# A layer's FFN with the up projection multiplied by seven products over its whole contraction, and the down projection in chunks of two pairs summed in device memory

## What is computed

```python
def conv_ffn(h, w_up, conv_w, conv_b, w_down):
    up = depthwise_conv(h @ w_up, conv_w, conv_b, FFN_CONV // 2)
    g, v = jnp.split(up, 2, axis=-1)
    return (jax.nn.gelu(g, approximate=True) * v) @ w_down
...
    hx2 = modulate(rms_norm(x, g_ffn_pre[l]), sh2, sc2)
    x = x + gt2 * rms_norm(conv_ffn(hx2, w_up[l], conv_ffn_w[l], conv_ffn_b[l], w_down[l]), g_ffn_post[l])
```

## Time and profile before

| what | value |
|---|---|
| median of 3 runs | 2086.96 us (2085.97 to 2090.21) |
| the profiled execution, its device time | 2088.77 us |
| its span, first to last instruction | 2087.0 us |
| PE busy | 98% of the span |
| DVE busy | 73% |
| ACT busy | 39% |
| mean granted TensorE clock | 0.995 |

### The profile page before, as it was taken

One profiled execution on the slowest core, in us unless ns is written; L12 is line 12 of the kernel. 1 busy time (PEld: TensorE's weight loads), 2 busy tenths in 40 slices (PEclk: granted clock), 3 DMA queues, 4 the chain that ended last, 5 costly groups with the idle time before them and its releaser, 6 DMA issues.

```text
span 2087.0 us, 28299 instructions
## 1 busy us (share of the span) xinstructions
PE 2054.5 (98%) x11682; PEld 1755.4 (84%) x11682; DVE 1528.3 (73%) x2203; ACT 812.1 (39%) x1078; POOL 78.7 (4%) x145
## 2 busy tenths in 40 slices
PE   7999999999999999999999999999999999999998
PEld 4678887888777888988889898898988888888887
DVE  5567978876889886776858676676776768577577
ACT  5346576543333352333424243242333424233243
POOL 0000000001110000000000000000000000000002
PEclk9999999999999999999999999999999999999999
DMA  9953424434886524333343433334333333333343
GB/s 393 408 213 111 145 92 168 136 112 155 328 286 238 172 91 142 101 122 121 102 141 102 131 111 105 128 111 132 107 117 124 102 128 103 99 101 101 101 180 104
DMA packets 86193, 311.19 MB, mean 149 GB/s; under 512 B 9456, under 2 KB 13552, under 8 KB 84016
## 3 DMA queue, kind: packets, MB, share of 16 engines
q1 hardware_dynamic: 67824, 243.09, 34.1%
q0 software_dynamic: 17424, 65.50, 9.5%
q10 hardware_dynamic: 816, 0.79, 0.1%
HBM read 300.95 MB, written 8.39 MB: 148 GB/s over the span
## 4 chain that ended last, share of the span: by engine, by line
PE 68%; DVE 2%; DMA 1%; issue 1%; ACT 0%; DVEq 0%; ACTq 0%
PE bank L1010 22%; PE bank L1011 22%; PE bank L1012 22%; DMA ada_raw<-in_adabg 1%; DVE w_lo L1554 0%; DVE acc L2191 0%; PE bank L1330 0%; PE bank L1121 0%; DVE ada_acc L1586 0%; DMA w_raw<-in_stream 0%; DVE x L1894 0%; ACT h_hi L622 0%; DVE prod L1905 0%; DVE ss L1562 0%; PE bank L1335 0%
## 5 line engine op out<-in xcount | busy, mean ns | idle before, releaser
L1010 PE MATMUL bank<-h_hi,w_hi 128*128 128x512 f32 (+1 forms) x1968 | 709.1, 360 | 4.5 <-ACT y_lru L691 1.1
L1011 PE MATMUL bank<-h_lo,w_hi 128*128 128x512 f32 (+1 forms) x1968 | 705.7, 359 | 0.0
L1012 PE MATMUL bank<-h_hi,w_lo 128*128 128x512 f32 (+1 forms) x1968 | 704.1, 358 | 0.0
L1554 DVE TENSOR_TENSOR w_lo<-w_raw,w_hi 128x1024 fp32r<-128x1024 f32 x260 | 315.9, 1222 | 151.2 <-ACT w_hi L622 150.6
L1010 PEld LDWEIGHTS bank<-h_hi,w_hi 128*128 128x128 f32 x1968 | 370.4, 188 | 62.6 <-issue 11.8
L622 ACT ACTIVATE w_hi<-w_raw 128x1024 fp32r<-128x1024 f32 x260 | 273.2, 1056 | 383.0 <-DMA w_raw<-in_stream 383.0
L1012 PEld LDWEIGHTS bank<-h_hi,w_lo 128*128 128x128 f32 x1968 | 370.4, 188 | 57.0
L1011 PEld LDWEIGHTS bank<-h_lo,w_hi 128*128 128x128 f32 x1968 | 370.7, 188 | 47.6
L1010 PE MATMUL bank<-act_hi,w_hi 128*128 128x512 f32 (+1 forms) x688 | 265.1, 385 | 1.8 <-DVE acc L2163 1.5
L1011 PE MATMUL bank<-act_lo,w_hi 128*128 128x512 f32 (+1 forms) x688 | 264.3, 384 | 0.0
L1012 PE MATMUL bank<-act_hi,w_lo 128*128 128x512 f32 (+1 forms) x688 | 264.3, 384 | 0.0
(11 more groups left out here) (340 smaller groups left out, 2704.4 us busy)
## 6 DMA issues: line engine op xcount, KB each, us to landing
w_raw<-in_stream SPq DMA_DIRECT2D x340, 512.0 KB, 3.5
ada_raw<-in_adabg POOLq DMA_DIRECT2D x112, 512.0 KB, 4.5
ada_raw<-in_ada SPq DMA_DIRECT2D x64, 512.0 KB, 13.8
x<-in_x_t SPq DMA_DIRECT2D x4, 1024.0 KB, 8.4
acc<-in_adabg SPq DMA_DIRECT2D x8, 512.0 KB, 6.0
x<-in_x_t POOLq DMA_DIRECT2D x4, 1024.0 KB, 8.8
x_kept_d<-x SPq DMA_DIRECT2D x4, 1024.0 KB, 5.6
c<-in_ctx_t SPq DMA_DIRECT2D x2, 1024.0 KB, 14.2
```

Of the source, the lines that this page charges most:

```text
L1010: t.matmul(out, w, v, start=start, stop=False)
L1011: t.matmul(out, w, v_l, start=False, stop=False)
L1012: return t.matmul(out, w_l, v, start=False, stop=stop)
L1554: v.tensor_tensor(lo_unit(n), raw_unit(n), hi_unit(n).bitcast(F32), ALU.subtract).then_inc(lo_done, 1)
```

## The change

- The up projection of pairs 4 to 43 uses seven products for all 16 feature tiles: four units of `seven_products` and none of `four_tiles`. The token sums are made for all eight couples of tiles (upper four couples first), in place in `acc` (one of them in `kick_raw`), with `t_lo` in the same room. `acc` is thereby taken until the last up unit. DVE no longer waits for `x1_kept` there; ACT does.
- DVE makes block sums for every up unit (three sets of room for them, `SETS`), and the ring has five slots throughout.
- The down projection goes in 20 chunks of two pairs, and a last one of four. Chunks 0 and 1 run whole behind pairs 4 and 5; from pair 6 to pair 41 eight tiles (half a chunk) run behind every pair, none behind pairs 42 and 43. A tile is 2 x 3 matmuls of 512 tokens. A unit of down weights holds four tiles.
- A finished tile is no longer added by DVE: ACT copies it from PSUM to one of four staging places (`take_down`), and POOL issues a DMA to device memory, a plain one for chunk 0 and one that accumulates after that (`add_down`). ACT may write a staging place again when the DMA from it has landed (`tile_moved`), and PE may write the bank when ACT has copied (`down_added`).
- In `seven_products` PE waits bank by bank for the copies of the tiles behind the pair before.
- The convolution is split in `convolve_gate` and `convolve_value` with other work between; `common_sums` of a pair waits for the pair's last unit where it waited for the third.
- At the end SP reads the sums back to `acc` (`load_sums`, 4 x 1 MB, after the last up unit is used), ahead of the four kept units.

```diff
-        WSUM[UP[_c, _p] + 1], WSUM[UP[_c, _p] + 2] = 0, 1
+QUADS = ((4, 5), (6, 7), (0, 1), (2, 3))
+SETS = 3
+WSUM = {UP[_p] + _w: 4 * (_p - CH) + _w for _p in range(CH, FT) for _w in range(4)}
...
+            def load_sums():
+                sp.wait_ge(*used(LAST_DOWN - 1))
+                for i in range(4):
+                    sp.wait_ge(tile_moved[i], 16 + 16 * (TILES // 4))
+                for i in range(4):
+                    sp.dma_start(acc[:, ds(4 * i * L, 4 * L)].rearrange("p (k l) -> p k l", k=4), acc_d[:, 4 * i:4 * i + 4, :]).then_inc(quarter_in[i], 16)
...
+                if n == UNITS - KEPT:
+                    load_sums()
                 load_unit(n)
...
+            def add_down(t, c, m):
+                pool.wait_ge(down_added, t + 1)
+                if c == 0:
+                    pool.dma_start(in_stage(acc_d[:, m, :]), stage(t % 4)).then_inc(tile_moved[t % 4], 16)
+                else:
+                    pool.wait_ge(tile_moved[t % 4], 16 + 16 * (t // 4))
+                    pool.dma_start(in_stage(acc_d[:, m, :]), stage(t % 4), accum_op=ALU.add).then_inc(tile_moved[t % 4], 16)
...
+            def take_down(n, t):
+                act.wait_ge(down_done, t + 1)
+                if t >= 4:
+                    act.wait_ge(tile_moved[t % 4], 16 + 16 * (t // 4))
+                a.activation(stage(t % 4), in_stage(bank[DOWN_BANK(n, t)][:, :]), ACT.Copy).then_inc(down_added, 1)
+            taken = 0
+            for n in range(CH, FT):
+                u, d = UP[n], AFTER_UP[n]
+                seeds_of(n - 1)
+                hi(u + 3)
+                gelu_of(n - 1)
+                hi(u + 4, u + 5)
+                round_of(n - 1)
+                hi(u + 6)
+                copy_first(n)
+                for unit in d:
+                    for t in range(taken, taken + 2):
+                        take_down(n, t)
+                    hi(unit + 3)
+                    for t in range(taken + 2, taken + 4):
+                        take_down(n, t)
+                    taken += 4
...
+                def bank_free(i):
+                    if first and free:
+                        pe.wait_ge(down_added, free - i)
...
+                    if ab == 0:
+                        bank_free(3)
+                    product(alone_v[:, 0:H], block_of(n, 6 + ab), t_of(q, 2), first and ab == 0, last and ab == 1)
+                    if ab == 0:
+                        bank_free(2)
+                    product(common[:, 0:H], block_of(n, ab), b11, first and ab == 0, False)
+                    if ab == 0:
+                        bank_free(1)
+                    product(alone_g[:, 0:H], block_of(n, 2 + ab), b21, first and ab == 0, False)
...
-            dve.wait_ge(x1_kept, 16 * 4)
-            for q in range(4):
-                k = KT // 2 + 2 * q
+            for half in range(2):
+                q0 = 4 - 4 * half
+                for q in range(q0, q0 + 4):
...
+            for n in range(CH, FT):
+                u, d = UP[n], AFTER_UP[n]
+                lo(u + 2)
+                if n > CH:
+                    if not AFTER_UP[n - 1]:
+                        common_sums(n - 1)
+                    pair_sums(n - 1)
+                sum_blocks(u + 3)
+                convolve_gate(n - 1)
+                lo(u + 3)
+                sums_if(u + 4)
+                convolve_value(n - 1)
+                lo(u + 4)
+                sums_if(u + 5)
+                multiply(n - 1)
+                lo(u + 5)
+                split_act(n - 1, (n - 1) % CH)
+                sums_if(u + 6)
+                for unit in d:
+                    sums_if(unit + 3)
+                    lo(unit + 2)
+                    if unit == d[0] and n in ADA_PAIRS:
+                        eat_ada(1)
+                    if unit == d[-1]:
+                        common_sums(n)
```

More of the change, by code:

```diff
@@ L92 @@
 BY_PE = 2 * len(SUM_BANK)
-DOWN_TILE = {DOWN[_c] + _u: KT * _c + 2 * _u + 2 for _c in range(NCH) for _u in range(KT // 2)}
 COUNT = {}
@@ L928, in gelu_of, with round_first @@
                 a.activation(cg[:, n % 2, :], cg[:, n % 2, :], ACT.Gelu_apprx_tanh).then_inc(ffn_gelu, 1)
+            def round_first(half):
+                q0 = 4 - 4 * half
+                act.wait_ge(*used(UP[FIRST] + 1 + 2 * half))
+                a.activation(first_of_two(h_hi[:, 2 * q0:2 * q0 + 8, :]), quarters_of[:, q0:q0 + 4, 1, :], ACT.Copy).then_inc(t_rounded, 1)
             for n in range(FIRST):
@@ L1389, in four_tiles, with product, seven_products @@
                 mm.then_inc(unit_used, 1)
-            def seven_products(n, w, b):
+            def product(out, block, x, start, stop):
+                return three(out, *block, *x, start, stop)
+            def seven_products(n, w, b, free):
                 alone_g, alone_v, common, parts = (bank[i] for i in b)
@@ L1395, in seven_products @@
                 _, high, low = sums_of(n)
-                def product(out, block, x, start, stop):
-                    return three(out, *block, *x, start, stop)
+                first, last = w == 0, w == 3
                 def sum_block(i, ab):
@@ L1410, in seven_products @@
[L1410 to L1421 removed]
+                    q = QUADS[w][ab]
@@ L1440, in down @@
[L1440 to L1454 removed]
+                    pe.wait_ge(t_ready, 3)
+                elif not AFTER_UP[n - 1]:
+                    pe.wait_ge(sum_v, n - 1 - CH)
@@ new lines, in up_pair, with down @@
+                for w in range(4):
+                    if n == CH and w == 2:
+                        pe.wait_ge(t_ready, 4)
+                    seven_products(UP[n] + w, w, UP_BANK(n), TILES_BY[n - 1] if n > CH and AFTER_UP[n - 1] else 0)
+            def down(n, taken):
+                if n == CH:
+                    pe.wait_ge(conv_v, CH)
+                else:
+                    pe.wait_ge(sum_v, n - CH)
+                if n in FFN_SUM:
+                    sum_ada(FFN_SUM[n], bank[7])
+                for i, (c, m) in enumerate(down_after(n)):
+                    t, u = taken + i, DOWN[c, m]
+                    pe.wait_ge(ffn_split, TWO * c + TWO)
+                    if m % 4 == 0:
+                        pe.wait_ge(lo_done, u + 1)
+                    if i >= 4:
+                        pe.wait_ge(down_added, t - 3)
+                    if i == 3 and n in FFN_SUM:
+                        pe.wait_ge(ada_read, FFN_SUM[n] + 1)
+                    for k in range(TWO):
+                        q = (TWO * c + k) % CH
+                        mm = three(bank[DOWN_BANK(n, t)][:, :], *block_of(u, TWO * (m % 4) + k), act_hi[:, q, :], act_lo[:, q, :],
+                                   k == 0, k == TWO - 1)
@@ L1455, in down @@
                     mm.then_inc(down_done, 1)
             for i, kg in enumerate((2, 3, 0, 1)):
[L1458 to L1465 removed]
+                four_tiles(UP[FIRST] + i, kg, UP_BANK(3), KT // 2, KT // 2 - 1)
+            for n in range(CH, FT):
+                up_pair(n)
+                if AFTER_UP[n]:
+                    down(n, TILES_BY[n - 1] if n > CH else 0)
@@ new lines, in sums_if @@
+            def sums_if(n):
+                if n in WSUM:
+                    sum_blocks(n)
+            for n in range(CH, FT):
+                u, d = UP[n], AFTER_UP[n]
[16 more added lines that the diff above has]
+                for unit in d:
+                    if unit == d[0] and n in FFN_SUM:
+                        take_ada(FFN_SUM[n], bank[7])
+                    sums_if(unit + 3)
[3 more added lines that the diff above has]
+                    if unit == d[-1]:
+                        common_sums(n)
@@ L2282 @@
         stream[OUT_H[m][0]], stream[OUT_H[m][1]] = w_out[m]
-    for c in range(NCH):
-        stream[DOWN[c]:DOWN[c] + 8] = w_down[c]
+    for c in range(CHUNKS):
+        for m in range(0, KT, 4):
+            stream[DOWN[c, m]] = by_two[c, m // 4]
+    stream[LAST_DOWN:] = by_four
     both = np.stack([w_up[:FIRST], w_up[FT:FT + FIRST]]).reshape(2, FIRST, 2, P, 2, 4 * P)
```

425 lines of the change are left out of this document (179 added, 246 removed).

## The result

The changed kernel takes 2229.34 us, median of 4 runs (2226.05 to 2242.32), beside 2086.94 us for the kernel before on the same chip: 1.0691 times as long, 95% interval 1.067 to 1.0713. Forecast were 2063 us and a range up to 2108. Rival A is what happened, and larger than its upper end.

A forecast was written before the change was run, and what follows sets the result against it. PE's matmul issue rate was taken to bound the kernel. Terms -53 + 2 + 3 + 2 + 12 + 2 + 8 = -24 us, against the median of 2086.96, gave 2063 us; range 2046 to 2108.

The forecast's parts named there:

- Rival A: Accumulating DMA lands late, holding ACT's copies and PE's 7th matmul of the next pair; 2107 to 2118 us, chance 0.29.
- the tiles' transfers: Accumulating DMAs of down tiles behind pairs: PE waits 0.1 us a pair, 3 us in all (0 to 58).
- L: Time from ACT's copy of a down tile to the landing of its DMA; put at 4.8 us.
- upper bound of 6.5: Highest landing time taken: load and store in a row, 3.3 + 2.2 + 0.3, and 0.7 for a stream load.
- The formula: PE waits not at all up to a copy-to-landing time of 4.9 us; beyond, 36 us for each us, over 36 pairs.
- The gain: Up projection, pairs 4 to 43: 48 matmuls of 512 become 84 of 256, 1.33 us a pair, 53 us saved.
- 2 off for pairs 42 and 43: No down tiles there to hide behind; DVE has 20.7 us of work for 19.1, costing 2 us (0 to 4).
- VectorE in the steady part: DVE's work per pair, 26.2 of 30.0 us, stays ahead of PE and costs nothing.
- The start: PE waits for DVE: 6.4 us ahead of pair 3, 4.6 at pair 4, 1 after; together 12 (8 to 15).
- The clock: A stall of 6 us at the start may lower the granted clock; 2 us (0 to 4).
- The end: After the last up unit, 4 MB of sums delay the kept units; pair 43's chain shows 2 us; 8 (5 to 11).
- C: Start and end hidden better than thought, with the low ends of all terms; 2047 us, chance 0.08.

The follow-up runs named there:

- experiment 4: Changed kernel with its 304 accumulating transfers taking the same bytes from a constant area in pieces of 2 KB instead of 1 KB; 2132.7 us, 1.0213 of the kernel before.
- experiment 5: Changed kernel with all 304 additions run from a constant area, so ACT need not wait for landings; 2051.82 us, 0.9821 of the kernel before.
- experiment 1: Changed kernel without the 304 accumulating transfers and the waits of ACT and GpSimd for them; 2051.93 us, 0.9825 of the kernel before.
- experiment 6: Changed kernel, whole computation, with eight down tiles behind a pair made four behind its second and four behind its fourth unit, one pair later; 2062.07 us, 0.9876.

## Why the prediction was wrong

**The term that failed is the tiles' transfers**, "L = 4.8, at the edge", 3 us with bounds 0 to 58. It measured 176 us (1362.6 - 1186.5). The mechanism was the right one and stood there as rival A: a landing holds a copy, the copy a bank, the bank PE's matmul of the next pair. For the first transfer of a burst L came out as forecast, 4.9 us. But the path goes through the second, and its L is 7.9, beyond the upper bound of 6.5. That bound was a load and a store in a row for one transfer on a busy queue, and its rows were of the wrong kind. The last step put an accumulation nearest to a 512 KB load by GpSimd because it moves as many bytes. No row of before had an addition in it, and an addition takes 2.4 to 2.9 times a store's engine time. What was left out is that more additions of 2.0 us of all engines each are under way before the second has landed. A bound has to be built for the burst.

**The formula gave the first part of the cost, and the holes brought more.** From the start of copy 1 to the start of copy 5 is the copy's own 0.60 and L, with less than 0.1 from the landing to the next copy. Over the 36 bursts it is 8.62 us on average in the changed kernel and 6.50 in experiment 4, so L is 8.0 and 5.9 (in the runs where ACT does not wait it is 5.44 from start to start, ACT's own pace). The formula gives 36 x 3.1 = 112 us and 36 x 1.0 = 36; measured were 176 and 82 (1268.5 - 1186.5). It lacks two things. In experiment 4 copy 6 starts within 0.2 us of the landing of the third transfer in all 36 bursts, so that landing and not the second's is the one that ends last: copy 6 ends 9.6 us after copy 1 where 8.0 costs nothing, which is 59 us. And in the changed kernel the granted clock is 0.96 on average from 800 to 2153, 0.04 x 1353 = 54 us at most. PE's waits for ACT's copies come to 94.9 us in 74 places there and to 55.7 in 41 in experiment 4. The rest of either is the slower pace of some pairs, some 10 us, and open.

**The gain** is there: -50.4 in the middle without additions. The middle has 39 of the 40 pairs, 52 of the 53 us, and the forecast took 2 off for pairs 42 and 43: -50. A pair takes 30.0 us as forecast, of it 168 matmuls in 19.0 and 48 in 10.9.

**VectorE in the steady part** cost nothing, as forecast: in the window 1300 to 1500 of experiment 5 it is busy 161 of 200 us, 81%, and PE never waits for it there.

**The start** was forecast at 12 + 2, and with pair 4's gain of 1.3 in that stage at 12.7. It measures 7.8, and 6.5 in experiment 1. Its steps, in the changed kernel:

```profile
744.22 0.80 PE L1081 MATMUL bank<-h_hi,w_hi 128*128 128x512 f32 x1 [6.39 <-DVE w_lo L1633]
...
770.43 0.36 PE L1081 MATMUL bank<-kick_hi,w_hi 128*128 128x256 f32 x1 [2.31 <-DVE sums_lo L1631]
776.02 0.39 PE L1081 MATMUL bank<-t_hi,w_hi 128*128 128x256 f32 x1 [0.55 <-DVE sums_lo L1631]
```

6.4 ahead of pair 3 came as 6.39. The 4.6 ahead of pair 4 came as 2.31 and the 1 behind it as 0.55. The clock took the 2 us that were set down for it: it is 0.66 from 744.2 to 750, which is 2.0 us of 5.8. And PE came to pair 3 at 737.8, 2.7 us ahead of the 740.5 of the kernel before; why is not shown, and it hides a part of the cost.

**The end** was forecast at 8 us (5 to 11) and measures 5.4 in the changed kernel and 7.1 in experiment 1. It came as forecast. ACT, VectorE and PE behind the last up unit, which is used by 2153.07:

```profile
2167.00 1.06 ACT L680 ACTIVATE h_hi<-x 128x1024 fp32r<-128x1024 f32 x1 [4.46 <-DMA x<-in_stream]
```
```profile
2168.09 1.22 DVE L1633 TENSOR_TENSOR h_lo<-x,h_hi 128x1024 fp32r<-128x1024 f32 x1 [3.08 <-ACT h_hi L680]
```
```profile
2163.32 0.50 PE L1081 MATMUL bank<-act_hi,w_hi 128*128 128x512 f32 x1 [1.88 <-DVE act_lo L2081]
...
2174.67 0.36 PE L1081 MATMUL bank<-act_hi,w_hi 128*128 128x256 f32 x1 [2.94 <-DVE acc L2239]
```

The kept units landed in 12.8 us in place of 6.7. ACT stood 4.5 us for the first, and its roundings ended 18.7 us after 2153.07, in the 18 to 21 of the forecast; VectorE stood for ACT, and PE for VectorE's addition of a last tile, 2.9 us. The wait of 1.9 is the chain of pair 43, forecast at 2.

**The spread of chances.** Rival A had 0.29, worked from an L of up to 6.5. C had 0.08, and 2052 us without the additions is near its 2047. The bounds of 0 to 58 us, for an operation that no row showed, were the widest of the sum and still did not hold. The range's upper end also does not follow from its own sum: at L = 6.1 the term is 43 us and the time 2103, and 2108 belongs to an L of some 6.2.

## What to carry to other kernels

A DMA that adds into memory is not a store with a little more: before a kernel leans on its landing, count its engine time for the burst in which it comes, not for one alone. Where only its landing hurts, the cure is not fewer transfers but more time until the buffer is written again; the same 304 additions were worth -1.2% when they came four at a time, and +6.9% eight at a time.

## What the runs showed of the hardware

- An accumulating DMA of 256 KB into device memory takes all 16 engines 1.65 us with pieces of 2 KB and 2.02 with pieces of 1 KB, a plain store 0.69. GpSimd is held 0.88 and 1.19 us by its issue, and 0.72 by the store's. From the end of the copy the first of a burst lands after 4.5 and 4.9 us, the second after 5.8 and 7.9; the stores after 2.9 both.
- Of the additions with pieces of 1 KB (272 packets each) at most three are under way: each of the 304 is issued after the third one back has landed. With pieces of 2 KB (144 packets, experiment 4) four were under way after 176 of the issues. The cause is open.
- A DMA share of 0.90 over 200 us beside a PE that is busy 200 of 200 costs PE nothing, as long as nothing waits for a landing (experiment 5).
- Holes of 1.8 and 1.5 us on PE were followed by windows of 2 us with a granted clock of 0.55 and 0.60, and starts 0.21 us apart, the lower level of 1.2 GHz for most of them. With two holes a pair in the changed kernel the mean granted clock from 800 to 2153 is 0.96, with one a pair in experiment 4 it is 0.99 from 800 to 2058; experiments 1, 5 and 6, nearly without holes, had 1.00, 2.4 GHz, through that stage.
- The short matmuls have two paces at the same granted clock, 0.1133 and 0.1176 us, each kept over 84 or 168 of them. Neither met waits nor a matmul of another size changed it; the cause is open.
